# Late columns of the modulation product in the first half feed-forward, and gating work in the maxima round

## The reference, cut to what matters

```python
def adaln(cvec, w_mod, b_mod):                 # first block: 6 x 1024 columns
    return jnp.split(jax.nn.silu(cvec) @ w_mod + b_mod, 6, axis=-1)

def spatial_gating(h, w_gm, v_gain, w_s, b_s): # first block, beside attention
    u, vv = jnp.split(jax.nn.gelu(h @ w_gm, approximate=False), 2, axis=-1)
    vv = rmsnorm(vv, v_gain).reshape(b, n // CHUNK, CHUNK, N_GM_GROUPS, GM_GROUP_DIM)
    mixed = jnp.einsum('gij,bcjgd->bcigd', w_s, vv) + b_s.T[:, :, None]
    return u * mixed.reshape(b, n, D_GM)
...
def ada_params(cvec, w, b):                    # second block: 9 x 1024 columns
    return (jax.nn.silu(cvec) @ w + b).reshape(cvec.shape[0], N_ADA, 1, D_MODEL)

def half_ffn(h, shift, scale, gate, g_pre, g_post, w13, w2):
    u = modulate_2(rmsnorm_2(h, g_pre), shift, scale)
    return h + 0.5 * gate * rmsnorm_2(swiglu(u, w13, w2), g_post)
...
h_lat = half_ffn(h_lat, ml[:, 0], ml[:, 1], ml[:, 2], g[0], g[1], w13_a[l], w2_a[l])
h_ctx = half_ffn(h_ctx, mc[:, 0], mc[:, 1], mc[:, 2], g[0], g[1], w13_a[l], w2_a[l])
h_lat, h_ctx_new = token_mixing(h_lat, h_ctx, (ml[:, 3], ml[:, 4], ml[:, 5]), (mc[:, 3], mc[:, 4], mc[:, 5]), ...)
h_lat = half_ffn(h_lat, ml[:, 6], ml[:, 7], ml[:, 8], g[4], g[5], w13_b[l], w2_b[l])
```

## Time and profile before

| | |
|---|---|
| median of 3 runs | 2324.3 us (2323.79 to 2329.31) |
| the profiled execution | 2324.03 us, span 2322.7 us |
| TensorE busy | 1988.2 us (86%) |
| VectorE busy | 1008.7 us (43%) |
| ScalarE busy | 735.0 us (32%) |
| GpSimd busy | 42.6 us (2%), 47 instructions |
| moved | 672.03 MB, mean 289 GB/s |
| mean granted TensorE clock | 0.930 |

### The profile page before, as it was taken

How to read it: one execution, slowest core, us unless ns; L and a number is a source line. 1 busy time by engine, 2 the same in 40 slices (tenths; PEclk the granted TensorE clock), 3 DMA queues, 4 the chain that set the end, 5 groups by cost and what they waited for, 6 DMA issues and landing times.

```text
span 2322.7 us, 28401 instructions
## 1 busy us (share of the span) xinstructions
PE 1988.2 (86%) x11830; PEld 1307.0 (56%) x11830; DVE 1008.7 (43%) x1713; ACT 735.0 (32%) x1196; POOL 42.6 (2%) x47
## 2 busy tenths in 40 slices
PE   6999877877877777877788789989999899999997
PEld 3646413433333333332444378868999788785786
DVE  3544222212222221222533277667664767653486
ACT  4323211101111111112210054454654554543365
POOL 0000000000000000000000000000000000000010
PEclk9999789899889998988889999999999999999999
DMA  9977999999999999999999965535345555350430
GB/s 390 414 306 266 408 377 413 414 413 414 413 414 416 415 413 415 414 411 409 414 403 410 410 207 181 186 102 169 113 141 177 164 178 186 98 199 19 145 119 19
DMA packets 210432, 672.03 MB, mean 289 GB/s; under 512 B 11504, under 2 KB 134512, under 8 KB 152192
## 3 DMA queue, kind: packets, MB, share of 16 engines
q1 hardware_dynamic: 210304, 670.21, 74.8%
HBM read 669.12 MB, written 1.05 MB: 289 GB/s over the span
## 4 chain that ended last, share of the span: by engine, by line
PE 50%; DMA 34%; DVE 11%; ACT 4%; issue 2%; SPq 0%; POOL 0%; DVEq 0%; ACTq 0%; POOLq 0%
DMA ring<-in_w 25%; PE pb L232 7%; PE pb L233 7%; PE pb L234 7%; PE pb L240 7%; DMA ring<-in_w_a 5%; PE pb L241 3%; PE pb L1852 3%; DVE WB L339 3%; DMA ring<-in_w_in 3%; PE pb L1877 2%; PE pb L782 2%; ACT WB L333 1%; DMA ring<-in_w_mod 1%; PE pb L1836 1%
## 5 line engine op out<-in xcount | busy, mean ns | idle before, releaser
L339 DVE TENSOR_TENSOR WB<-ring,WB 128x1024 fp32r<-128x1024 f32 (+3 forms) x370 | 426.1, 1193 | 463.9 <-ACT WB L333 463.6
L333 ACT ACTIVATE WB<-ring 128x1024 fp32r<-128x1024 f32 (+3 forms) x370 | 361.6, 1026 | 799.2 <-DMA ring<-in_w_a 466.0
L1852 PE MATMUL pb<-ring,big 128*32 128x512 f32 x2048 | 302.7, 684 | 139.9 <-DMA ring<-in_w 124.2
L232 PE MATMUL pb<-HHL,WB 128*128 128x256 f32 (+1 forms) x976 | 292.0, 299 | 11.7 <-DVE WB L339 4.3
L233 PE MATMUL pb<-HHL,WB 128*128 128x256 f32 (+1 forms) x976 | 283.0, 290 | 0.0
L234 PE MATMUL pb<-HHL,WB 128*128 128x256 f32 (+1 forms) x976 | 282.5, 289 | 0.0
L240 PE MATMUL pb<-HHL,WB 128*128 128x512 f32 x704 | 250.0, 400 | 1.9 <-DVE tmpT L649 1.5
L1852 PEld LDWEIGHTS pb<-ring,big 128*32 128x32 f32 x2048 | 47.3, 114 | 360.1 <-DMA ring<-in_w 268.3
L232 PEld LDWEIGHTS pb<-HHL,WB 128*128 128x128 f32 x976 | 194.0, 199 | 35.8 <-issue 21.3
L1877 PE MATMUL pb<-ring,big 128*32 128x512 f32 x1024 | 172.5, 673 | 48.4 <-DMA ring<-in_w 40.4
L241 PE MATMUL pb<-HHL,WB 128*128 128x256 f32 x704 | 197.3, 280 | 0.0
(11 more groups left out here) (467 smaller groups left out, 2265.0 us busy)
## 6 DMA issues: line engine op xcount, KB each, us to landing
ring<-in_w SPq DMA_DIRECT2D x384, 1024.0 KB, 16.4
ring<-in_w_a SPq DMA_DIRECT2D x66, 1024.0 KB, 13.2
ring<-in_w_in SPq DMA_DIRECT2D x38, 1024.0 KB, 10.2
ring<-in_w_ada SPq DMA_DIRECT2D x36, 1024.0 KB, 9.9
ring<-in_w_b SPq DMA_DIRECT2D x33, 1024.0 KB, 5.0
ring<-in_w_mod SPq DMA_DIRECT2D x24, 1024.0 KB, 12.0
ring<-in_w_out SPq DMA_DIRECT2D x8, 1024.0 KB, 6.3
ring<-in_b_w_in SPq DMA_DIRECT2D x8, 1024.0 KB, 6.4
```

The source lines that it names most:

```text
L232: pe.matmul(o, l[0], r[0], start=start, stop=False)
L333: act.activation(WB[:, c % 2, 0, x:y], flat[:, x:y], ACT.Copy).then_inc(*A(("high", c, z)))
L339: dve.tensor_tensor(WB[:, c % 2, 1, x:y], flat[:, x:y], WB[:, c % 2, 0, x:y].bitcast(F32), ALU.subtract).then_inc(*V(("low", c, z), *([("f ...
L1852: e = pe.matmul(PB[half][32 * j:32 * j + 32, :], xeT[:, kk, 32 * x:32 * x + 32], s[:, 512 * j:512 * j + 512], start=kk == 0, stop=kk == 7)
```

## The change

1. Of the 36 units of `w_ada_2`, 16 are taken out of the threaded vector products: the columns 5120 to 9216 (rows 5 to 8 of the parameters). `ADA` has two full groups and `TWO` (now columns 4096 to 5120). `FILL` gives the number of units after each projection chunk.
2. These 16 loads stand in SyncE's order between the chunks of `fa` (`LATE_AT`: after chunks 1, 2, 3, 5, 6, 7, 9, 10, 11, 13, 14, 15, 17, 18, 19, 21). ScalarE scales each by the column of silu(c) (`act_late`), GpSimd adds it to a total (`pool_late`), in two sets b of eight; for b = 1 the total lies in two places and each add is two instructions. TensorE sums each total over its partitions with a matrix of ones (`pe_late_sum`), ScalarE copies, TensorE picks the columns, VectorE adds the bias and makes the gains.
3. In the first block the squares, the root and the gain of `vv` go into the maxima round, as do the two gate rows; the mixing product of the first tile comes ahead of the value products, and the transposed scores of z = 1 ahead of the turning of the maxima.
4. The picks get a step of their own (`steps` hands back what the generator yields, and `next(g2)` takes it); the router's logits use bank 3 instead of 6.

```diff
@@ steps
-        if next(g, None):
-            break
+        end = next(g, None)
+        if end:
+            return end
@@ groups
-    ADA = [("ada", nb) for nb in range(5)]
-    TWO = ("ada", 4)
+    ADA = [("ada", nb) for nb in range(3)]
+    TWO = ("ada", 2)
+
+    FILL = (1, 1, 1, 1, 2, 2, 1)
@@ sp_gemv
-                    load(sp, (v, u), w[256 * u:256 * u + 256, 8192:9216].rearrange("(a p) n -> p a n", p=128), 2048, "p (a n) -> p a n", a=2)
+                    load(sp, (v, u), w[256 * u:256 * u + 256, 4096:5120].rearrange("(a p) n -> p a n", p=128), 2048, "p (a n) -> p a n", a=2)
@@ new functions
+    def late_columns(b, u):
+        w = I["w_ada_2"][0][128 * u:128 * u + 128, :]
+        return w[:, 6144:8192] if b else w[:, 5120:9216].rearrange("p (a n) -> p a n", n=1024)[:, 0:4:3, :]
+
+    LATE_AT = {1 + 4 * k // 3: k for k in range(16)}
...
+    def late_total(b):
+        return ((big[:, 6656:8192], 0, 1536), (mraw[:, :], 1536, 2048)) if b else ((big[:, 3584:5632], 0, 2048),)
+
+    def act_late(act, t):
+        if t not in LATE_AT:
+            return
+        b, u = divmod(LATE_AT[t], 8)
+        part = slot(("late", b, u))
+        act.wait_ge(*landed(("late", b, u)))
+        if u:
+            act.activation(part, part, ACT.Copy, scale=cs[:, 1, u, 0:1]).then_inc(*A(("late", b, u)))
+            return
...
+    def pool_late(pool):
+        for b in range(2):
+            for u in range(1, 8):
+                pool.wait_ge(*at("late", b, u))
+                pool.wait_ge(*(at("late_total", b, u - 1) if u > 1 else at("late", b, 0)))
+                for total, x, y in late_total(b):
+                    pool.tensor_tensor(total, total, slot(("late", b, u))[:, x:y], ALU.add).then_inc(
+                        *G(*([("late_total", b, u), ("free", ("late", b, u))] if y == 2048 else [])))
...
+    def pe_late_sum(pe, b):
+        pe.wait_ge(*at("late_total", b, 7))
+        pe.wait_ge(*at("summed", "fa", 9 if b else 6, 0 if b else 1, 0 if b else 1))
+        for j in range(4):
+            total = late_total(b)[j // 3 if b else 0][0]
+            e = pe.matmul(late_bank(b)[32 * j:32 * j + 32, :], ones[:, 0:32], total[:, 0:512] if b and j == 3 else total[:, 512 * j:512 * j + 512],
+                          start=True, stop=True)
+        e.then_inc(*P(("late_sum", b)))
@@ projections, SyncE, TensorE, ScalarE, VectorE
-                steps(g2, 3)
+                steps(g2, FILL[q - 1])
...
-            steps(g2, 3)
+            steps(g2, FILL[3 + q])
@@ maxima round, ScalarE
         for n in range(8):
+            if n == 1:
+                for i in range(2):
+                    act.wait_ge(*last("a"))
+                    act.activation(tmp_row[:, 0:512], gm[:, i, 512:1024], ACT.Square, scale=512 ** -0.5, accum_out=st[:, 40 + i:41 + i]).then_inc(*A(("squares", "vv", i)))
+                act_root(act, "vv", st[:, 40:42])
@@ maxima round, VectorE
+            if n == 7:
+                run(row)
+            if n in (9, 11):
+                i = n // 2 - 4
+                if i == 0:
+                    dve_rstd(dve, "vv", st[:, 40:42])
+                    dve.wait_ge(*last("v"))
+                vv = gm[:, i, 512:1024]
+                dve.scalar_tensor_tensor(vv, vv, st[:, 40 + i:41 + i], gains[:, 640:1152], ALU.mult, ALU.mult).then_inc(
+                    *V(("vv", i), *([("free", "gains")] if i else [])))
@@ sp_half
             load_chunk(sp, c)
+            if F is fa:
+                sp_late(sp, c - F.s0)
@@ pe_half
+                    if F is fa and (p, q, f) == (7, 1, 0):
+                        pe_late_sum(pe, 0)
+                    if F is fa and (q, f) == (1, 1) and p in (8, 10):
+                        pe.wait_ge(*at("late_raw" if p == 8 else "late_out", 0))
...
+            if F is fa and p == 9:
+                pe_late_pick(pe, 0)
@@ act_half
                         act.wait_ge(*at("summed", name, p, 0, f))
                         act.activation(F.sl[f], F.sl[f], ACT.Silu).then_inc(*A(("silu", name, p, f)))
+                if F is fa:
+                    act_late(act, 2 * p + q)
...
+            elif F is fa and p == 8:
+                act_late_raw(act, 0)
@@ pool_program
             pool_turn2(pool, name)
+            if name == "fa":
+                pool_late(pool)
```

More of the change, by code:

```diff
@@ L952, in pe_first @@
             if q:
-                steps(g2, 3)
+                if ended == 2:
+                    next(g2)
+                ended = steps(g2, FILL[q - 1])
             else:
@@ L982, in pe_first @@
             e.then_inc(*P(("used", 4 + q), *([("gm",)] if q == 3 else [])))
-            steps(g2, 3)
+            if ended == 2:
+                next(g2)
+            ended = steps(g2, FILL[3 + q])
             if q in (1, 2):
@@ L986, in pe_first, with gt_row @@
         turned(3)
+        def gt_row(z):
+            pe.wait_ge(*at("diagonals", "gt", z))
+            pe.wait_ge(*(at("rowed", "gt", 0) if z else at("gelu", 0, 0)))
+            pe.matmul(PB[6][:, :], ones, gt_diag, start=True, stop=True).then_inc(*P(("row", "gt", z)))
         for n in range(16):
@@ L995, in pe_first @@
                 *P(("scores1", n)))
[L996 to L1003, removed]
+            if ended == 2:
+                next(g2)
+            ended = steps(g2, 1) if n % 2 else 0
+            if n in (6, 10):
+                gt_row(n // 4 - 1)
         def scores(p, z):
@@ L1022, in pe_first, with mixing @@
         e.then_inc(*P(("m_turned",)))
-        gt_row(0)
+        if ended == 2:
+            next(g2)
         scores(0, 0)
-        scores(0, 1)
-        gt_row(1)
+        def mixing(i):
+            pe.wait_ge(*at("vv", i))
+            if i == 0:
+                pe.wait_ge(*landed("ws"))
+                pe.wait_ge(*at("rowed", "gt", 1))
+            else:
+                pe.wait_ge(*at("gated", 0))
+            for g in range(8):
+                e = pe.matmul(PB[6][:, 64 * g:64 * g + 64], slot("ws", 1024, "p (g i) -> p g i", g=8)[:, g, :],
+                              gm[:, i, 512 + 64 * g:576 + 64 * g], start=True, stop=True)
+            e.then_inc(*P(("mixed", i), *([("free", "ws")] if i else [])))
         pe.wait_ge(*at("mT"))
@@ L1062, in o_turned, with uv_turned @@
             e.then_inc(*P(("o_turned", g)))
+        mixing(0)
         def gating():
[L1065 to L1077, removed]
+            def uv_turned(i):
                 pe.wait_ge(*at("uv", i))
@@ L1307, in dve_first, with maxima @@
         dve.tensor_copy(mT, PB[4][0:8, 0:256]).then_inc(*V(("mT",)))
-        run(row)
-        for j in (1, 3):
+        def maxima(j):
             q = MBC[j]
```

119 lines of the change are left out of this document (89 added, 30 removed).

## The result

The changed kernel takes 2374.91 us (median of 4 runs, 2364.78 to 2382.80) against 2324.05 us; the ratio is 1.0212 with an interval of 1.0188 to 1.0236. It is slower, by 51 us. The forecast had the sign, with 2356.5 us, and its range ended at 2371. The profiled execution took 2379.43 us, 4.5 above the median; what that does to the readings ahead of the experts is told where the kernel before is profiled again.

A forecast was written before the change was run, and what follows sets the result against it. Weight transfers bound the experts, TensorE the part before 294.8 us and the gate and up loop of `fa`. Forecast: 2324.0 - 15.3 + 6.8 + 41 = 2356.5 us, range 2311 to 2371.

The forecast's parts named there:

- port term: In `fa`, GpSimd's 14 long adds hold VectorE's two-SBUF-input instructions and so TensorE: 41 us, bounds 0 and 64.
- gain ahead of the experts: Before the expert stream, fewer units, reordering, shorter routing and ready tiles bring 15.3 us, bounds 8 and 22.
- `w2` part: The part of `fa` behind the gate and up loop: adds were to make it 6 us longer.
- layout of 44 us: Paper schedule of `fa`, instruction by instruction: 51 us longer with adds, of which 44 is the port's.
- projections: Ten units fewer there free 9.3 us of TensorE, less 2.3 for a VectorE wait: 7.0 us gained, bounds 4.6 and 9.3.
- TensorE work is only moved: Reordering in first attention can only win back TensorE's idle time: 3.0 us, bounds 0 and 6.9.
- routing: Six units fewer between turned affinities and turned slots; TensorE then waits for VectorE's top-32 search, so 1.3 us gained.
- ready tiles: At the first expert product seven free slots can all hold expert tiles: 4 us gained, bounds 2 and 5.
- cost in `fa` without the port: Loads and scalings hidden, sums and picks on TensorE 3.8 us, a new wait at pair 8 3.0 us: 6.8 us together.
- Rival A: In `fa`, the long adds don't hold VectorE: 2315.5 us, faster; chance 0.17.
- Rival B: Adds don't hold VectorE, and the expert stream gains the full 41 us ceiling: 2290 us; chance 0.04.
- Rival C: Adds hold VectorE, but its slack takes two thirds: port 8 to 15 us, total 2324 to 2331 us; chance 0.10.

The follow-up runs named there:

- the kernel with fills: Changed kernel with each GpSimd add replaced by two fills of the same sums, so the late columns are not computed: 2319.80 us, ratio 0.9978 to the kernel before.

## Why the prediction was right in sign and short in size

Taken apart by these runs, the changed kernel is 2324 - 10 + 7.1 + 52.8 = 2374 us, against 2324.0 - 15.3 + 6.8 + 41 = 2356.5. Of the 18.4 us between 2356.5 and the measured 2374.9, the port term is 11.8, the gain ahead of the experts 5.3 and the rest of `fa` 0.3; 1 us is left over.

- **The port term (41, measured 52.8) is the step that failed, in size.** The mechanism was as laid out: without adds there is no loss, the adds hold VectorE's halves and products, and the reductions from PSUM don't take part (0.67 to 0.69 us each beside the adds). The 52.8 is a difference of two medians, 47 to 59 by the intervals of their ratios; the two traces have 49.2 in the loop and 2.6 in the `w2` part. The forecast called a layout of 44 us and took 41, "nearer to the whole hold". Two things were off. The layout had 44 us of waits alone, with TensorE at full clock, and put the clock at nothing without a reason; in the changed kernel's loop idle time grows by 32.1 - 4.5 = 27.6 us and busy time by 149.9 - 128.3 = 21.6 us, at a granted clock of 0.86 instead of 1.00. How much of the 21.6 us would be waiting for VectorE anyway, had the clock held, is open: slow products also hide waits. And the bound "with slower handing over 47" lies under the measured value; only the 64 us of "all of GpSimd's time" held it. VectorE's records are 42.5 us longer in the loop (131.97 for 89.43 us) and 2.9 in the `w2` part, with 50 forecast.
- **The gain ahead of the experts (15.3, measured 10, 6 in the profile)** is the second term that was off. The projections were right or better: 9 us for 7.0. "TensorE work is only moved, so what can come back is its idle time", set at 3.0, came to 1.3 us for the new order in one pair and 2.2 against it in the other, neither to be told from none; with the 1.3 for the routing, 4.3 us were forecast for a stretch that gives back 0 to 3 at a like clock. The ready tiles, set at 4.0, gave 1 to 2: the sixteenth tile lands 28.1 us behind the first expert product (27.7 to 28.9 in the eight profiles) for 29.9 before, and 26 was forecast. Seven tiles do lie ready, the last since 237.4 us, but then the ring is full and the queue stands still. Chain, SyncE's timeline and a window of the changed kernel:

```profile
246.87 8.52 PE pb L1976 x64
...
258.93 15.99 DMA ring<-in_w
...
248.79 0.33 SPq L226 DMA_DIRECT2D ring<-in_w  x1
...
237.40:254.30 16.90, 14.88 (x90) 9.06 (x90) 6.59 (x17) 1.51 (x4) 0.00 (x0) 0.64 0.26 84
```

  The eighth tile is asked for 2.0 us behind the first expert product and lands 5.5 us later, at 254.3; the forecast had 0.9 and 2.5. In the changed kernel's profile the lead of the first stage goes between 124 and 220 us, at the lower clock. The kernel before meets such stretches as well, and why the changed one loses more of its lead there is open; the forecast had counted TensorE's time at one fixed price. Where the clock holds better the forecast comes nearer: in the kernel with fills the first expert product is at 236.9 us (forecast 235) and `fa` starts 13.6 us sooner. Of the kernel before no such early profile was caught, so part of the 13.6 may be the scatter.
- **The cost in `fa` without the port (6.8, measured 7.1)** came out, part by part, within the 2 us that its profiles allow: 3.8 us of sums and picks, for which some 2.1 stand in the loop and 2.1 behind it, and the new wait at pair 8, forecast at 3.0, took 2.9 us with no adds and 4.0 with them.
- **The `w2` part** was to be 6 us longer and is 4.7.
- **Rival A** ("the long adds don't hold VectorE", 2315.5 us) is what the fills do: 2319.8. The 4 us between them fit the smaller gain ahead of the experts. It failed as a forecast because the adds do read SBUF and hold VectorE for as long as they last. **Rival B** asked for the full stream's ceiling: `fa` would start at 1306, and no profile has it under 1332. **Rival C**, that the slack takes two thirds of the port's cost, would need 8 to 15 us; even pieces of 256 columns cost 19 in the loop.

The loads were hidden, as forecast: share 0.82 at 287 GB/s in the loop of the kernel without adds, and no TensorE wait there on a transfer.

## What to carry to other kernels

Before giving GpSimd an elementwise job beside a busy VectorE, ask whether it reads SBUF while VectorE runs instructions with two inputs there: then its time is not free, and an add of 4.4 us cost 3.8 us of the kernel (52.8 / 14), while the same add on VectorE, where it takes 2.3 us, cost nothing that TensorE saw. Price such a job as VectorE's time first, and look at how long a single instruction holds, since here the half that was held was the one that TensorE waited for next. Count the clock too: 21.6 of the 49.2 us in the loop were slower products and not waits. Loads taken off ahead of a stream help only as far as the ring can hold what then comes early, here seven tiles. And before reading a gain or a loss of a few microseconds out of one profile, compare it with a second profile of the same instructions: here two of them differ by 10 us ahead of the experts.

## What the runs showed of the hardware that was not expected

- A GpSimd copy (one SBUF operand) holds a VectorE instruction with two as an add does: a half of 1.22 us took up to 2.92 us beside copies of 2.1 to 2.3 us in the mean. Fills of 1.8 us left every half at 1.22 to 1.23.
- Cutting an add into eight pieces lowers its cost in the loop from 49.2 to 19.2 us, not to an eighth. GpSimd's busy time in the loop rises from 70.2 to 108.1 us. In part it is held too: its pieces of 256 columns have a median of 0.74 us and a maximum of 1.72. In part pieces are dearer by themselves: eight of 0.72 us, the shortest seen, are 5.7 us, for an add of 4.4.
- The same instructions, in step within 0.1 us for 124 us, came to run at a granted clock of 0.50 in one execution and 0.99 in another from 140 to 150 us, with TensorE busy throughout in both. What decides it no run here shows.
